# Half of an output projection inside a threshold search, and a GpSimd that forms low weights

## The reference, cut to what matters

```
h = rmsnorm(x) * (1 + scale1) + shift1 ;  P = h @ w_in        # q, k, v, indexer, SSD, pooling inputs
A = attention over the 256 keys with the largest indexer scores (512 columns)
B = SSD mixer (256 columns) ;  C = pooling mixer (256 columns)
x = x + gate1 * (concat[A, B, C] @ w_out)                     # w_out: 1024 x 1024
x = x + gate2 * SwiGLU(rmsnorm(x) * (1 + scale2) + shift2)
```

## Time and profile before

| | us |
|---|---|
| median of the three runs | 3217.33 |
| the three runs | 3209.84, 3218.40, 3217.33 |
| span of the profiled execution | 3218.5 |
| mean granted TensorE clock over it | 0.967 |

### The profile page before, as it was taken

The page is one execution under the profiler, slowest core; times in us unless marked ns, Lnnn a source line. Parts: engine busy times, 40 slices in busy tenths (PEclk is TensorE's granted clock), DMA queues, the critical chain, the costliest instruction groups (busy, mean ns, idle before and its releaser), DMA issues.

```text
span 3218.5 us, 56238 instructions
## 1 busy us (share of the span) xinstructions
PE 3014.0 (94%) x20185; PEld 2635.5 (82%) x20185; DVE 1604.0 (50%) x3493; ACT 1334.5 (41%) x2398; POOL 262.7 (8%) x334
## 2 busy tenths in 40 slices
PE   7999878889999999999989997889899999999998
PEld 5899433558999999999989963346599999999998
DVE  4565699764722322322556567986474222222234
ACT  4433688665522122122443247866564211211234
POOL 1012321011000000000000141100300000000000
PEclk8999989989999999999999998999899999999999
DMA  6622365026311111111432343620642111111124
GB/s 201 163 65 69 108 236 184 2 100 196 99 52 43 48 46 43 48 46 46 116 89 55 69 131 132 209 92 2 230 129 63 45 46 50 46 42 52 46 72 139
DMA packets 356491, 293.60 MB, mean 91 GB/s; under 512 B 85288, under 2 KB 319206, under 8 KB 356024
## 3 DMA queue, kind: packets, MB, share of 16 engines
q1 hardware_dynamic: 325036, 186.21, 19.8%
q0 software_dynamic: 31152, 104.76, 10.5%
q10 hardware_dynamic: 108, 0.11, 0.0%
HBM read 273.33 MB, written 9.78 MB: 88 GB/s over the span
## 4 chain that ended last, share of the span: by engine, by line
PE 64%; DVE 6%; issue 3%; ACT 2%; DMA 1%; POOL 0%; DVEq 0%; ACTq 0%; POOLq 0%; SPq 0%
PE bank L859 44%; PE bank L876 11%; PE bank L843 2%; DVE arena L2635 2%; PE bank L1436 1%; PE bank L1410 1%; DMA arena<-in_cache_v,page_idx 1%; PE bank L917 1%; ACT arena L1902 1%; DVE w_lo L2107 1%; PE bank L1241 0%; PE bank L1370 0%; PE bank L1499 0%; POOL arena L725 0%; ACT w_hi L1629 0%
## 5 line engine op out<-in xcount | busy, mean ns | idle before, releaser
L859 PE MATMUL bank<-h_hi,w_hi 128*128 128x352 f32 x2736 | 891.7, 326 | 11.7 <-DVE arena L2261 7.2
L859 PE MATMUL bank<-h_lo,w_hi 128*128 128x352 f32 x2736 | 880.0, 322 | 0.0
L859 PE MATMUL bank<-h_hi,w_lo 128*128 128x352 f32 x2736 | 879.2, 321 | 0.0
L2107 DVE TENSOR_TENSOR w_lo<-weights,w_hi 128x1024 fp32r<-128x1024 f32 x250 | 306.4, 1225 | 678.0 <-ACT w_hi L1629 671.5
L859 PEld LDWEIGHTS bank<-h_hi,w_hi 128*128 128x128 f32 x2736 | 515.9, 189 | 17.2 <-issue 13.7
L859 PEld LDWEIGHTS bank<-h_lo,w_hi 128*128 128x128 f32 x2736 | 516.5, 189 | 0.3
L859 PEld LDWEIGHTS bank<-h_hi,w_lo 128*128 128x128 f32 x2736 | 515.2, 188 | 0.0
L1629 ACT ACTIVATE w_hi<-weights 128x1024 fp32r<-128x1024 f32 x250 | 264.1, 1056 | 453.3 <-PE bank L859 294.6
L843 PEld LDWEIGHTS bank<-arena 128*128 128x128 f32 (+2 forms) x1717 | 199.3, 148 | 163.3 <-issue 95.3
L843 PE MATMUL bank<-arena 128*128 128x128 f32 (+2 forms) x1717 | 271.1, 290 | 46.1 <-ACT arena L1939 15.8
L876 PE MATMUL bank<-g_hi,w_hi 128*128 128x352 f32 (+2 forms) x768 | 255.7, 333 | 11.1 <-DVE arena L767 5.4
(11 more groups left out here) (396 smaller groups left out, 4369.6 us busy)
## 6 DMA issues: line engine op xcount, KB each, us to landing
arena<-in_w_ada SPq DMA_DIRECT2D x96, 512.0 KB, 4.5
weights<-in_w_down SPq DMA_DIRECT2D x48, 512.0 KB, 3.9
weights<-in_w_gate SPq DMA_DIRECT2D x44, 512.0 KB, 3.8
weights<-in_w_up SPq DMA_DIRECT2D x44, 512.0 KB, 3.8
weights<-in_w_in SPq DMA_DIRECT2D x66, 256.0 KB, 3.8
weights<-in_w_down SPq DMA_DIRECT2D x32, 448.0 KB, 3.6
weights<-in_w_out SPq DMA_DIRECT2D x96, 128.0 KB, 2.9
weights<-in_w_out SPq DMA_DIRECT2D x48, 256.0 KB, 3.1
```

Source lines behind the costliest of these rows:

```text
L859: mm = pe.matmul(bank[:, 0:TC], wt[:, w], xt[:, x], start=(k + m == 0), stop=(k == n_k - 1 and m == 2))
L2107: dve.tensor_tensor(w_lo[:, w], S(O_W + n % 2 * UNIT, UNIT), w_hi[:, w].bitcast(F32), ALU.subtract).then_inc(unit_lo, 1)
```

## The change

In 24 passes (layer 0: passes 1, 3, ... 31 for blocks 0 and 1; layer 1: passes 17, 19, ... 31 for block 0) PE also multiplies the lower half of `w_out` for one output tile and one block, as plain fp32: four matmuls into a bank of its own. SP loads those weights (256 KB, for two blocks at once in layer 0). DVE adds the result to x one pass later, behind the count of set 6. In the output projection the units of these blocks keep only tiles 0 to 3: 12 matmuls, two DMAs with 256 KB, a high part half as wide, and a low part formed by GpSimd. To free a PSUM bank, `keys` now turns the same half of two key tiles in each pass and multiplies both one pass later, in neighbouring column groups. Scratch areas are moved, with waits that keep them apart.

```diff
+EARLY = (2, 1)
+def early_at(l, i):
+    first = 1 if EARLY[l] == 2 else 17
+    if i < first or i % 2 == 0:
+        return None
+    q = (i - first) // 2
+    return q, q // EARLY[l], q % EARLY[l]
 # SP
+                def early_unit(m):
+                    if m:
+                        sp.wait_ge(early_done, early_base(l) + EARLY[l] * m)
+                    settle(sp)
+                    sp.dma_start(V(O_EARLY, [[P, 4], [1, P]]), wo[512:1024, m * P:m * P + P].rearrange("(i p) n -> p i n", p=P)).then_inc(early_full, 16)
                 for u in range(4 * KD):
+                    m, rest = divmod(u - (1 if EARLY[l] == 2 else 17), 2 * EARLY[l])
+                    if rest == 0 and m >= 0:
+                        early_unit(m)
...
+                    unit(n, *heads, *(rest if u // KD >= EARLY[l] else ()))
 # GpSimd, behind its last gather
+                for u in range(KD * EARLY[l]):
+                    done = l * LAYER_UNITS + N_IN + u
+                    w = slice(u % 2 * UNIT, u % 2 * UNIT + 4 * P)
+                    pool.wait_ge(unit_hi, done + 1)
+                    pool.tensor_tensor(w_lo[:, w], S(O_W + u % 2 * UNIT, 4 * P), w_hi[:, w].bitcast(F32), ALU.subtract).then_inc(unit_lo, 1)
 # PE
+                def keys(s):
+                    for j in range(2):
+                        keys_turned(s, j)      # half s % 2 of tile s // 2 * 2 + j
+                    if s:
+                        key_logits(s - 1)      # both tiles
+                def early_product(i):
+                    if early_at(l, i) is None:
+                        return
+                    q, m, c = early_at(l, i)
+                    if c == 0:
+                        pe.wait_ge(early_full, (l * KD + m + 1) * 16)
+                    if early_base(l) + q:
+                        pe.wait_ge(early_read, early_base(l) + q)
+                    for k in range(4):
+                        mm = pe.matmul(GB[:, 0:TC], S(O_EARLY + P * k, P), S(H(4 + k, c * TC), TC), start=(k == 0), stop=(k == 3))
+                    mm.then_inc(early_done, 1)
                     modulate(O_ADA[i % 2], i % (2 * KD) // 2, i % 2).then_inc(w_empty, 1)
+                    early_product(i)
...
+                        Dr.close(product_part(bank, j, c * TC, TC, g_hi, g_lo, True, ..., n_k=4 if c < EARLY[l] else KD))
 # DVE
+                def early_added(i):
+                    ...
+                    dve.wait_ge(early_done, early_base(l) + q + 1)
+                    x = S(O_X + m * TOK + c * TC, TC)
+                    dve.scalar_tensor_tensor(out=x, in0=GB[:, 0:TC], scalar=S(O_MOD + 9 * (2 * KD + m), 1), in1=x,
+                                             op0=ALU.mult, op1=ALU.add).then_inc(early_read, 1)
                             if i > 5 and i % 4 == 2:
                                 logits_in((i - 6) // 4)
+                            early_added(i - 1)
+                        if j == 1 and i:
+                            dve.wait_ge(count_raw, l * (PASSES + 1) + (i + 1))
+                        if j == 2:
+                            dve.wait_ge(dve_step, step.count.at(-1))
...
-                split_lo(0)
-                for k in range(KD):
-                    gate_lo(l, 0, k, 0, TC)
+                out_lo(0)                      # nothing while u // KD < EARLY[l]
+                for k in range(4):
+                    gate_lo(l, 0, k, 0, TC, 1 if k < 3 else KD - 3)
```

More of the change, by code:

```diff
@@ L865, in product, with product_part @@
                 units.n += 1
-            def product_part(bank, n, x0, wide, hi, lo, used=False, tiles=None, first=0):
-                for k in range(KD):
+            def product_part(bank, n, x0, wide, hi, lo, used=False, tiles=None, first=0, n_k=KD):
+                for k in range(n_k):
                     if tiles is not None:
@@ L875, in product_part @@
                     for m, (wt, xt) in enumerate(((w_hi, hi), (w_hi, lo), (w_lo, hi))):
-                        mm = pe.matmul(bank[:, 0:wide], wt[:, w], xt[:, x], start=(k + m == 0), stop=(k == KD - 1 and m == 2))
+                        mm = pe.matmul(bank[:, 0:wide], wt[:, w], xt[:, x], start=(k + m == 0), stop=(k == n_k - 1 and m == 2))
                         if used and k + m == 0:
@@ L1347, in _, with keys_turned @@
                 settle(pe)
-                A.restart()
+                A.use(AB_FEW)
                 evicted, logit_banks = {}, {}
-                def keys_turned(h):
-                    n, half = h // 2, h % 2
+                def keys_turned(s, j):
+                    n, half = s // 2 * 2 + j, s % 2
                     if half == 0:
@@ L1360, in keys_turned @@
                     A.close(mm)
[L1361 to L1382, removed]
+                    evicted[s] = A.count.n
+                def key_logits(s):
+                    half = s % 2
+                    A.wait_read(A.count.n - evicted[s])
+                    for i in range(2):
+                        n = s // 2 * 2 + i
+                        gq, j = n // 16, n % 4
+                        if j == 0:
+                            logit_banks[half] = Dr.open()
+                        mm = pe.matmul(B(logit_banks[half], [[1, 512]], 0, 32 * j, 32), S(O_QB + 32 * (4 * gq + j), 32), S(O_KT[(2 * s + i) % 4], 512),
+                                       start=True, stop=True)
+                        if half == 0:
+                            mm.then_inc(s_kv_used, 1)
+                        elif j == 3:
+                            Dr.close_all(mm, 2)
@@ L1537, in _ @@
                         bank = Dr.open()
-                        Dr.close(product_part(bank, j, c * TC, TC, g_hi, g_lo, True, norm.tile_lo - 2 * KD if c + j == 0 else None))
+                        Dr.close(product_part(bank, j, c * TC, TC, g_hi, g_lo, True, norm.tile_lo - 2 * KD if c + j == 0 else None,
+                                              n_k=4 if c < EARLY[l] else KD))
                         units.n += 1
@@ L1892, in keys_copied @@
                         bank = A.next()
-                        A.done(act.activation(S(O_KT[h % 3], 512), bank[:, :], ACT.Copy))
+                        A.done(act.activation(S(O_KT[h % 4], 512), bank[:, :], ACT.Copy))
                 for i in range(PASSES):
@@ L2850, in _, with out_lo @@
                 sample_rows(0)
-                split_lo(0)
-                for k in range(KD):
-                    gate_lo(l, 0, k, 0, TC)
+                def out_lo(u):
+                    if u // KD < EARLY[l]:
+                        units.n += 1
+                        return
+                    if u == KD * EARLY[l]:
+                        dve.wait_ge(unit_lo, units.at(2))
+                    split_lo(u)
+                out_lo(0)
+                for k in range(4):
+                    gate_lo(l, 0, k, 0, TC, 1 if k < 3 else KD - 3)
                 sample_rows(1)
```

78 lines of the change are left out of this document (48 added, 30 removed).

## The result

The changed kernel takes 3239.55 us, the median of four runs (3237.02 to 3243.24), against 3217.27 for the kernel before in the same measurement; the ratio is 1.0070, 95% interval 1.0056 to 1.0083. It is slower by 22 us, where 4 were forecast. The profiled execution took 3241.85 us, its span 3240.1.

What follows compares the result with a forecast made beforehand. PE was taken to bound the output projection, DVE the search with PE close behind. Search +27.3 us and projection -23.0 summed to +4.3 on 3217.3, giving 3221.6 us; the 8-in-10 range was 3201 to 3237.

Steps and rivals of the forecast that it cites:

- DVE's additions, +12.0: Search: 24 additions out of PSUM at 0.50 us each on DVE, which bounds the pass, with nothing hiding them; +12.0 us.
- The waits behind set 6, +16.8: Search: DVE waits for the early product, ten times 1.4 us and eleven times 0.25 behind `logits_in`; +16.8 us.
- The search's tail, nothing: End of each search: the two last additions stand in the tail and were given no wait.
- Gathers in pairs, nothing: Search: gathers released in pairs, with two to three passes of lead (8 to 12 us), cost nothing.
- The smaller relief, -1.5: Search: turned keys' second half reaches ACT a microsecond sooner, saving some 0.1 us in one pass of four; -1.5 us.
- Block 0, -9.0 and -7.5: Output projection, block 0: shortened units at 2.8 us instead of 3.83; -9.0 us in layer 0, -7.5 in layer 1.
- The clock in block 0, to hold at 1.00: Output projection, block 0: units of 1.91 us every 2.8 keep PE's granted clock at 1.00 (2.4 GHz).
- Block 1, -3.5 between 0 and -7.8: Layer 0's projection, block 1: saves 7.8 us without GpSimd-DVE conflict; half a conflict, 0.75 us in six steps, leaves -3.5.
- Ahead of the projection, -1.5 twice: Before each layer's projection: half a megabyte less on saturated DMA saves 1.5 us, twice; -3.0 us (0 to -4).
- Rival 2: Search: DVE never waits for the early product behind set 6; -14 to -17 us, 3206 us; chance 0.22.
- Rival 3: Projection: GpSimd and DVE exclude each other, slowing block 1 and block 0; +9 us, 3230 us; chance 0.20.
- Rival 4: Search: modulation weights load late behind the early product, 1 us in each of 15 passes; 3237 us; chance 0.10.

Runs made afterwards that it cites:

- experiment 5: Changed kernel plus three fp32 matmuls of 256 columns adding zeros on PE in search passes without an early product; 3230.42 us, ratio 1.0044.
- experiment 4: Changed kernel with its loads and early products, but DVE neither waits for nor adds them (sum left out of the output); 3201.96 us, ratio 0.9949.
- experiment 3: Changed kernel with the lower half of those blocks left out altogether: no loads, products or additions in the search; 3192.62 us, ratio 0.9929.
- 1: Changed kernel with DVE's early addition moved from behind set 6 to behind the tallies of sets 6, 0, 1 and 2; 3211.94 us, ratio 0.9984.
- experiment 6: Changed kernel with the addition behind sets 6, 0, 1, 2 and layer 0's products in passes 3, 5 to 15, 16, 17 to 31; 3215.10 us, ratio 1.0005.
- 7: The kernel of experiment 6 plus three zero-adding filler matmuls on PE in passes without an early product; 3217.22 us, ratio 0.9995.
- experiment 10: The best version plus three zero-adding filler matmuls on PE in the passes without a product; 3210.62 us, ratio 0.9979.
- experiment 8: The kernel of experiment 6, but DVE forms the shortened units' low weights and GpSimd does nothing in the projection; 3215.66 us, ratio 0.9993.
- 2: Changed kernel with key tiles in pairs and new scratch areas only: no early products or additions, all projection units whole; 3213.65 us, ratio 0.9995.
- the best version: Changed kernel with the addition behind sets 6, 0, 1, 2, layer 0's products in passes 3, 5 to 31, sixteenth behind the last; 3210.20 us, ratio 0.9977.

## Why the prediction was wrong

The time came out above the range of 3201 to 3237. The sum of the terms was right in kind, and the mechanism of each was found in the trace; one term was half of what it should have been, one that was put at nothing cost 5 us, and one reading was wrong and did no harm, by luck.

- *DVE's additions, +12.0*: right. The addition at 457.92 is followed by the next tally at 458.42, 0.50 later, 24 times.
- *The waits behind set 6, +16.8*: this is the step that failed; it measured 34.5. At the full clock the single waits were right (1.35 for 1.4, 0.15 for 0.25), and so was their alternation. Over the 24 additions, 13.2 us came on top from passes at the half clock (1.7, 1.6, 3.2 and 1.5 us in layer 0; 0.9, 1.6 and 2.8 in layer 1), and 5.9 at the first product. The filler (experiment 5) shows for the seven steady ones that it was the clock; of the first product's 5.9, 2.9 depend on when the half clock at the search's start ends. I had worked out that PE has a microsecond less to do for a pair and that DVE's pass gets longer, and did not draw the line from there: PE then has nothing to do for 2.3 us in every second pass, where it had 0.2 to 1.4 in each before. I asked whether the clock would hold in the projection's block 0, where it did (1.00 from 791.8 to 820.0), and never in the search. The chain feeds itself: DVE waits, so the next count is late, so PE idles longer, so the clock falls, so the next product is late. Without the wait (experiment 4) the pauses are 1.7 us at most and the clock holds. The bound of 35 was reached, by another cause than the one it stood for (logits one after the other; they run side by side: both are done in 1.06 us, from 453.83 to 454.89, where one alone took 1.05 before).
- *The search's tail, nothing*: +5.2, which the prediction left out. Behind the last pass DVE waits for PE's last logits, 1.76 us in layer 0 and 3.40 in layer 1. Before, it didn't wait there; with the pairs alone it waits 0.96 and 0.98, with products but no additions 1.68 and 1.63.

```profile
591.86 0.75 DVE L2806 TENSOR_SCALAR arena<-arena,code 128x1024 f32<-128x1024 f32 x1 [1.76 <-PE bank L1407]
...
2159.58 0.75 DVE L2806 TENSOR_SCALAR arena<-arena,code 128x1024 f32<-128x1024 f32 x1 [3.40 <-PE bank L1407]
```

- *Gathers in pairs, nothing*: right in the steady search, wrong at layer 0's start. There two tiles, the modulation's weights and the product's weights land together and PE is still at the half clock; pass 2 took 11.89 us (before 4.60), the product 4.56. Product and load stand for 4.3 of it, by experiments 3 and 4 as by 1 and 6.
- *The smaller relief, -1.5*: 4.7 us for both searches with the pairs alone, 6.6 when the 1.9 of their tail are set apart. So the search comes to 12.0 + 34.5 + 5.2 - 6.6 = 45.1, against 45.4 measured.
- *Block 0, -9.0 and -7.5*: -8.8 and -8.8. From the projection's first matmul to the residual of the eighth unit layer 0 took 31.7 us and takes 22.9. In layer 1 some 2 us of it are the half clock that before's first unit had the earlier trace rows and this execution's didn't. The second unit comes 4.1 us behind the first, the others every 2.3 to 3.2, and the chain of waits is the ring that was described, to the term (5.65 us for two units, from one SP issue to the same one two units on; forecast 5.6):

```profile
802.46 0.59 SPq L557
...
803.10 2.82 DMA weights<-in_w_out
...
806.03 0.64 ACT w_hi L1680
...
806.73 1.29 POOL w_lo L780
...
808.11 0.60 SPq L557
```

- *The clock in block 0, to hold at 1.00*: it held, and that was luck. The earlier trace rows are no units with gaps: they are pieces of one chain, with PE's other work between them, and the window beside them has PE busy for 40.00 of 40.00 us. So no row said anything on a PE that pauses, neither for block 0 nor for the search. In block 0 PE was busy 22.95 of 28.20 us at 1.00:

```profile
791.80:820.00 28.20, 22.95 (x127) 19.98 (x126) 18.00 (x30) 17.30 (x34) 12.64 (x10) 1.00 0.32 94
```

  In the profiled executions of experiments 7 and 10 it fell in the same block, with the same code (0.83 from 5 to 15 us), and in six of the ten it fell from 15 to 30 us behind the start of layer 1's projection.
- *GpSimd's subtraction, taken as 1.2*: 1.28. The 4497 ns for 2048 elements in the Trainium skill, GPSIMD Engine Reference, Performance versus the Vector engine, are 1.12 for 512 in proportion, an estimate, and not the 1.2 that the prediction names; the measured operation is 14% above it.
- *Block 1, -3.5 between 0 and -7.8*: -6.3 (33.1 to 26.8). The conflict is there and cost 1.5 us, not 4.5, if the 7.8 without it were right, which no run shows. DVE's operations with two SBUF inputs that start while GpSimd works are held until it is done, as experiment 8 shows; the trace agrees with the rule of the Trainium skill, SBUF — State Buffer, Who interferes with whom, on those operations, and on the addition out of PSUM, which is not held. What I over-priced is how often they meet: a step of 2.75 us holds one GpSimd operation of 1.28, and part of DVE's work there is of the other kind or waits anyway. Five of the eight operations met one of DVE's in this block and held it, for 2.6 us in all.
- *Ahead of the projection, -1.5 twice*: -4.2 and -1.5, but not shown. The pairs alone, with whole loads, have -2.5 and -2.3 there, and layer 1's attention scatters by 8 us with the same code.

Rival 2 (DVE never waits) was wrong in this kernel, and is nearly made true by moving the addition. Rival 3 is real as a mechanism and small. Rival 4 gave the nearest time (3237) for a reason that didn't occur; it occurred in experiment 6. By the stages the change costs +45.4 - 5.7 - 22.3 = +17.4 us; the forecast had +27.3 - 3.0 - 20.0 = +4.3; the index stage's clock accounts for the 4.1 between that and the span's 21.6.

Put together: relieving the projection is worth 21 us (experiment 3 against 2), the products and their loads in the search ask some 7 (the searches of 4 against those of 3; the medians differ by 9), the additions 12 (0.50 each in the timeline), and the place of the addition another 28. In the best version little is left of the 21: it is 3 us below the pairs alone, which is no more than the scatter.

## What to carry to other kernels

Work moved into a stage that another engine bounds is free only if nobody there waits for it: put its consumer as late in the bound engine's pass as its operands allow, before counting what it costs. When an edit makes PE's share of a pass shorter, look where the new pause falls and what PE must deliver right behind it; a pause of 2 us can cost more than the microsecond that was saved (0.9 to 3.2 us for one product here). A load put on a queue behind a wait for a product delays every load behind it, so a product that is displaced by one pass can stop the stage (5.2 us here).

## What the runs showed of the hardware that was not expected

In the searches the clock fell with pauses of 1.8 to 2.5 us that recur every two to four passes, but only with some of them: in the changed kernel ahead of four products of layer 0; with another pause of 2.31 us, which ends at 462.66, it stayed at 1.00:

```profile
462.66 0.38 PE L1380 MATMUL bank<-arena 128*128 128x1 f32 x2 [2.31 <-DVE arena L2712]
```

(0.38 us for the count, 0.58 at the half clock.) With three fp32 matmuls of 256 columns in the pause (1.57 us) it held. Why one pause of 2.31 us brings a fall and the next doesn't stays open. The clock in the index stage and in layer 1's attention differs between the profiled executions as well; that attention took 187.3 to 195.8 us in the kernels measured, with the same code. A kernel's runs spread over 6 to 20 us, and the longer ones have the lower granted clock: in experiment 10 the shortest, 3202.48 us, has a mean of 0.966, the longest, 3221.96, one of 0.959. Differences of 3 us are read from stages, not from totals.

A DVE operation held by GpSimd ends at a fixed distance behind it, whenever it started: 0.38 us for 352 elements and 0.75 for 704, in all 18 cases of the changed kernel. Alone these operations take 0.52 and 0.89, so only the first 0.14 of them runs beside GpSimd's. One that started before GpSimd's kept its 0.57.
